# Strassen's seven block products in the second feed-forward layer

## The chip, the core and the metric

One core of a Trainium2 chip runs the program. Its engines work side by side, each from its own instruction stream, and meet through semaphores: TensorE (PE in the profile; PEld is its weight load) multiplies matrices into PSUM banks, VectorE (DVE) and ScalarE (ACT) do elementwise work, GpSimd (POOL) is nearly unused here, SyncE (SP) issues the weight loads. The metric is the device time of one execution in microseconds.

## The reference, cut to what matters

Two transformer stacks follow one another on 512 tokens of width 1024, all in fp32. The change is in the last feed-forward layer of the first stack:

```
h      = rms_norm(x) * gain              # [512, 1024]
gate   = h @ w_gate                      # [1024, 2816]
up     = h @ w_up                        # [1024, 2816]
hidden = silu(gate) * up                 # [512, 2816]
x      = x + hidden @ w_down             # [2816, 1024]
```

A final norm (`final_gain`) follows, and its output is the input of the second stack. Feed-forward layer 0 has the same shape and is not touched.

## The kernel before, in words

Activations are kept transposed: a tile is 128 features (the partitions) by 512 tokens. `x` and `h` have 8 tiles, `hidden` has 22 (FT). A weight block of 128 by 128 is the stationary operand, the tokens stream past it: one fp32 matmul of 512 columns (tokens), or of 256 for half of them. In the trace each fp32 matmul is two records, each with its weight load.

**Weights** come through a ring of 5 slots of 1 MB (`Ring`, L123, `Slot`, L108). SyncE issues the loads in order (L117), each as soon as the instruction that last read the slot has counted. A gate/up slot holds one tile: 8 blocks of the gate and 8 of the up projection. A down slot holds 16 blocks.

**Gate/up** is `GatedUnits` (L271). A unit is (tile, first token, last token): tiles 0 to 2 are done in two halves (6 units of 256 tokens), so that the low half can start before the high half of the norm is there, then tiles 3 to 21 with all 512 tokens. A unit is 16 matmuls (L295): 8 into a gate bank, 8 into an up bank, two such pairs of banks in turn. ScalarE takes Silu of the gate bank (L304) and VectorE multiplies by the up bank into `hidden` (L309). Unit u waits for the multiply of u - 2.

**Down** is `OutProjection` (L212): 10 units, 6 tiles of 512 tokens, then tiles 6 and 7 in their low and in their high half; 22 matmuls each (L254). VectorE adds each result to `x` (L268).

**Norms** (`Norm`, L140): for each unit of `x` ScalarE squares (L160), TensorE adds up over partitions with a matrix of ones (`sum`, L172), ScalarE takes the root (L182), VectorE a reciprocal and one refining step (`factor`, L188 to L196) and then 8 outputs (L202), low and high half of the tokens apart. The final norm's squares and sums run beside the down units; the factor of the low half starts after the ninth unit of ten (the sum of the eighth), the high half after the last.

The order of work is written out by hand, one stream for each engine. On TensorE the stretch ends

```
                    gate.unit(pe, 0)
                    norm.sum(pe, 11)
                    for n in range(1, len(gate.units)):
                        gate.unit(pe, n)
```

and `down_stage` then runs units 0 to 9 of the down projection, each followed by the norm sum of the unit before. VectorE runs the adds 0 to 8, `factor` and the outputs of the low half, add 9, and `factor` and outputs of the high half. When all is done, the second stack starts on every engine (at 1670.3 us of the profiled execution).

Of the kernel before, what the change touches and what calls it, by code (L numbers as in the profile page):

```python
# [13 lines left out]
P = 128  # L14
# [125 lines left out]
class Norm:  # L140
# [22 lines left out]
    def sum(self, pe, u):  # L163
        t, lo, hi = self.units[u]
        s = (self.number + u) % 4
        after(pe, self.squared, u)
        if t == 0 and self.chain.start:
            pe.wait_ge(self.chain.sem, self.chain.start)
        both = [(0, lo, hi)] if self.banks[0] == self.banks[1] else [(n, max(lo, i), min(hi, j)) for n, (i, j) in enumerate(SPANS)]
        for n, i, j in both:  # L170
            if i < j:
                m = pe.matmul(self.k.bank[:, self.banks[n], i:j], self.k.ones, self.squares[:, s, i:j],  # L172
                              start=(t == 0), stop=(t == self.tiles - 1))
        m.then_inc(self.summed.sem, 1)

# [95 lines left out]
class GatedUnits:  # L271


    def __init__(self, k, ring, norm, h, hidden, silu):
        self.k, self.norm, self.h, self.hidden, self.silu_ = k, norm, h, hidden, silu
        self.units = ([(t, 0, HALF) for t in range(3)] + [(t, HALF, SEQ) for t in range(3)]
                      + [(t, 0, SEQ) for t in range(3, FT)])
# [4 lines left out]
        self.slots = [ring.place((self.done, max(u for u in range(n) if self.units[u][0] == t))) for t in range(FT)]  # L282
# [23 lines left out]
    def multiply(self, v, u):  # L306
        t, lo, hi = self.units[u]
        after(v, self.silued, u)
        v.tensor_tensor(self.hidden[:, t, lo:hi], self.k.bank[:, 2 * (u % 2) + 1, lo:hi], self.silu_[:, u % 2, lo:hi],  # L309
                        ALU.mult).then_inc(self.product.sem, 1)  # L310

# [382 lines left out]
def first_block(k, x, h, a, constants, vectors, ctx_mod, sigmoid):  # L694

    vec = k.vec
    with ExitStack() as stack:
        ring = Ring(k, stack, 5, 100)
# [162 lines left out]
        norm3, gated1, down1 = ffn(out1, vec["norm_ffn1"], 38, {})  # L861
        norm4 = Norm(k, "final", x, KT, down1.units, [(down1.added, i) for i in range(10)], vec["final_gain"], x, (7, 6), temps, 50)
# [94 lines left out]
        with k.nc.Block(no_gpsimd_drain=True) as block:  # L957
            @block.sync
            def _(sp):
# [66 lines left out]
                for t in range(FT):  # L1026
                    gated1.slots[t].fetch(sp, a["gu1"][t])
                for i in range(11):
                    down1.slots[i].fetch(sp, a["down1"][i])
# [20 lines left out]
            def _(pe):  # L1050
                def mixer_end(out, norm, gate, group):
# [15 lines left out]
                    for i in range(8, 11):  # L1067
                        norm.sum(pe, i)
                    gate.unit(pe, 0)
# [51 lines left out]
                mixer_end(out0, norm1, gated0, ada_group)  # L1121
# [27 lines left out]
                mixer_end(out1, norm3, gated1, lambda n: None)  # L1149
                down_stage(down1, norm4, lambda: None)  # L1150
                norm4.sum(pe, 9)

            @block.scalar
            def _(e):
                def mixer_end(norm, gate):
# [6 lines left out]
                    norm.root(e, 1)  # L1162
                    for n in range(1, len(gate.units)):
                        gate.silu(e, n)

# [40 lines left out]
                mixer_end(norm1, gated0)  # L1206
                down_stage(norm2)
# [16 lines left out]
                down_stage(norm4)  # L1224
                norm4.root(e, 1)

            @block.vector
            def _(v):
                def mixer_end(out, norm, gate, group):
# [9 lines left out]
                    for t in range(KT):  # L1239
                        norm.out(v, 1, t)  # L1240
                    for n in range(1, len(gate.units)):
                        gate.multiply(v, n)
                        group(n)

# [75 lines left out]
                mixer_end(out0, norm1, gated0, ada_rows)  # L1320
# [43 lines left out]
                mixer_end(out1, norm3, gated1, lambda n: None)  # L1364
                down_stage(down1, norm4, lambda: None)
# [2185 lines left out]

def halves(w):
# [13 lines left out]
def layout(i):  # L3566
# [20 lines left out]
    for j in range(3):  # L3587
# [24 lines left out]
        "gu0": gu[0], "gu1": gu[1], "down0": stream(i["ffn_w_down"][0]), "down1": stream(i["ffn_w_down"][1]),  # L3612
# [21 lines left out]
```

## Time and profile before

| | |
|---|---|
| median of 3 runs | 3064.34 us (3064.19 to 3064.74) |
| profiled execution, span | 3059.0 us |
| instructions in it | 31313 |
| TensorE busy | 94% of the span |
| VectorE, ScalarE busy | 26%, 16% |

The profile is of one execution; its span runs from its first to its last instruction. The median of the runs stands 5.3 us above it. L is a line of the kernel. A group's row gives busy time, mean duration of one instruction in ns, and the engine's idle time before them with what ended it. Matmuls are pipelined, so their durations overlap.

### The profile page before, as it was taken

Reading aid. Unit: us, or ns where it says so; the run is one execution under the profiler, and the core shown is the slowest. Engines: PE = TensorE matmul, PEld = TensorE weight load, DVE = VectorE, ACT = ScalarE, POOL = GpSimd, SP = SyncE. Lnnn points to the kernel's source line nnn. Section 1 sums busy time; section 2 is a strip of 40 time slices with the busy share of each in tenths; the row PEclk is TensorE's granted clock in tenths of the full one; section 3 lists DMA queues with packets and bytes.
Section 4 is the critical chain, followed back from the end, with each engine's and each line's share of the span. In section 5 each row is a group of like instructions: output and inputs, shape, how many; then the busy total and the mean of one; then the engine's idle time right before and its main releaser. Section 6 shows DMA issues by size and latency. Waiting matters only on the chain. (4 is left out here: it accounts for less than half of the span.)

```text
span 3059.0 us, 31313 instructions
## 1 busy us (share of the span) xinstructions
PE 2888.6 (94%) x13580; PEld 1501.2 (49%) x13580; DVE 792.2 (26%) x1577; ACT 498.4 (16%) x1045; POOL 101.0 (3%) x90
## 2 busy tenths in 40 slices
PE   7998999999999999999998999789969989996998
PEld 4343475444455447544446745788623334432332
DVE  2325531010003233000002274555221231112113
ACT  2333310000001231000001231443110010001001
POOL 1000000000010010000000200010000000000000
PEclk9999999999999999999999999998989999997999
DMA  7211036545221111222111201100099953009994
GB/s 244 93 42 42 28 115 262 218 180 220 82 85 69 68 66 56 87 78 83 69 69 60 111 29 59 34 23 2 23 399 419 419 207 145 14 6 395 419 420 193
DMA packets 68577, 430.81 MB, mean 141 GB/s; under 512 B 8042, under 2 KB 8857, under 8 KB 21464
## 3 DMA queue, kind: packets, MB, share of 16 engines
q1 hardware_dynamic: 63640, 412.48, 34.5%
q0 software_dynamic: 4800, 16.33, 1.5%
q8 instruction: 107, 1.75, 0.2%
q14 instruction: 30, 0.25, 0.0%
HBM read 422.33 MB, written 13.79 MB: 143 GB/s over the span
## 5 line engine op out<-in xcount | busy, mean ns | idle before, releaser
L295 PE MATMUL bank<-h,weight_ring 128*128 128x512 f32 (+1 forms) x1600 | 608.3, 542 | 0.0
L295 PEld LDWEIGHTS bank<-h,weight_ring 128*128 128x128 f32 x1600 | 303.1, 190 | 300.3 <-issue 290.4
L254 PE MATMUL bank<-arena,weight_ring 128*128 128x512 f32 (+1 forms) x1264 | 422.9, 491 | 0.0
L254 PEld LDWEIGHTS bank<-arena,weight_ring 128*128 128x128 f32 x1264 | 238.1, 190 | 170.5 <-issue 154.5
L2151 PE MATMUL bank<-weight_ring,tokens_T 128*64 128x512 f32 x1024 | 231.8, 603 | 1.5 <-issue 1.5
L906 PE MATMUL bank<-h,weight_ring 128*128 128x512 f32 (+2 forms) x464 | 183.1, 547 | 5.2 <-DVE h L202 3.4
L2638 PE MATMUL bank<-h,weight_ring 128*128 128x256 f32 (+1 forms) x576 | 172.9, 457 | 8.5 <-ACT h L1933 8.5
L309 DVE TENSOR_TENSOR arena<-bank,arena 128x512 f32<-128x512 f32 (+1 forms) x50 | 31.4, 627 | 557.3 <-ACT arena L304 557.3
L3286 PE MATMUL bank<-h,weight_ring 128*128 128x512 f32 x384 | 166.6, 597 | 3.7 <-DMA weight_ring<-in_sc_in 3.7
L2151 PEld LDWEIGHTS bank<-weight_ring,tokens_T 128*64 128x64 f32 x1024 | 77.0, 139 | 153.0 <-issue 147.6
L2638 PEld LDWEIGHTS bank<-h,weight_ring 128*128 128x128 f32 x576 | 109.5, 192 | 70.6 <-issue 55.9
L906 PEld LDWEIGHTS bank<-h,weight_ring 128*128 128x128 f32 (+1 forms) x464 | 86.9, 193 | 96.2 <-issue 90.1
L304 ACT ACTIVATE arena<-bank 128x512 f32<-128x512 f32 (+1 forms) x50 | 27.3, 546 | 613.0 <-PE bank L295 613.0
L2190 PE MATMUL bank<-logits_or_select,h 128*128 128x512 f32 x256 | 118.7, 600 | 2.9 <-DVE logits_or_select L2311 2.9
L3286 PEld LDWEIGHTS bank<-h,weight_ring 128*128 128x128 f32 x384 | 73.5, 192 | 96.2 <-issue 91.2
L2174 PE MATMUL bank<-weight_ring,hidden_T 128*64 128x512 f32 x512 | 113.4, 595 | 3.4 <-DVE hidden_T L2299 3.1
L906 PE MATMUL bank<-weight_ring,h 128*128 128x512 f32 x256 | 113.5, 597 | 0.0
L268 DVE TENSOR_TENSOR x<-bank,x 128x256 f32<-128x256 f32 (+1 forms) x44 | 24.0, 545 | 338.0 <-PE bank L254 338.0
L160 ACT ACTIVATE arena<-x 128x512 f32<-128x512 f32 (+1 forms) x52 | 27.3, 530 | 387.4 <-DVE x L268 370.3
L400 DVE COPY arena<-bank 128x512 f32<-128x512 f32 x96 | 61.8, 685 | 93.5 <-PE bank L409 64.9
L906 PEld LDWEIGHTS bank<-weight_ring,h 128*128 128x128 f32 x256 | 47.6, 190 | 62.5 <-issue 58.7
L2318 DVE SCALAR_TENSOR_TENSOR x<-bank,vectors,x 128x512 f32<-128x512 f32 x80 | 60.1, 751 | 67.0 <-PE bank L2190 65.9
(387 smaller groups left out, 2633.0 us busy)
## 6 DMA issues: line engine op xcount, KB each, us to landing
weight_ring<-in_w_gate SPq DMA_DIRECT2D x64, 1024.0 KB, 25.0
weight_ring<-in_w_up SPq DMA_DIRECT2D x64, 1024.0 KB, 26.3
weight_ring<-in_w_down SPq DMA_DIRECT2D x64, 1024.0 KB, 26.1
arena<-in_ada_w SPq DMA_DIRECT2D x48, 1024.0 KB, 9.1
weight_ring<-in_gu SPq DMA_DIRECT2D x44, 1024.0 KB, 4.8
weight_ring<-in_down SPq DMA_DIRECT2D x22, 1024.0 KB, 4.8
weight_ring<-in_sc_in SPq DMA_DIRECT2D x12, 1024.0 KB, 12.2
weight_ring<-in_ev_in SPq DMA_DIRECT2D x8, 1024.0 KB, 6.9
```

The lines of the kernel that those rows point to most:

```text
L160: a.activation(self.squares[:, s, lo:hi], self.src[:, t, lo:hi] if src is None else src, ACT.Square, scale=(self.tiles * P) ** -0.5).then_ ...
L254: m = pe.matmul(bank, self.slots[i].buf[:, at * P:(at + 1) * P], self.src(c)[:, lo:hi], start=(c == 0), stop=(c == self.kt - 1))
L295: m = pe.matmul(self.k.bank[:, 2 * (u % 2) + p, lo:hi], self.slots[t].buf[:, at:at + P], self.h[:, c, lo:hi], start=(c == 0), stop=(c == K ...
L309: v.tensor_tensor(self.hidden[:, t, lo:hi], self.k.bank[:, 2 * (u % 2) + 1, lo:hi], self.silu_[:, u % 2, lo:hi], ALU.mult).then_inc(self.p ...
L400: v.tensor_copy(self.prob_T[:, c % 2, s, :], self.k.bank[:, 4 + s, :]).then_inc(self.copied.sem, 1)
L906: m = pe.matmul(out, lhs, rhs, start=(c == 0), stop=(c == last - 1))
L2151: m = pe.matmul(self.k.bank[e * CAP:(e + 1) * CAP, 3 + j, :], self.tok_T[:, r % 2, 4 * half + c, e * CAP:(e + 1) * CAP], slot.buf[:, c * D ...
L2174: m = pe.matmul(self.k.bank[e * CAP:(e + 1) * CAP, 6 + half, :], self.hid_T[:, 2 * fh + f, e * CAP:(e + 1) * CAP], slot.buf[:, at:at + 512 ...
L2190: m = pe.matmul(self.k.bank[:, 2 if n % 2 == 0 else 5, :], self.y[:, self.place(r), c * P:(c + 1) * P], self.sel[:, self.place(r), :], sta ...
L2318: v.scalar_tensor_tensor(self.x[:, c, :], self.k.bank[:, 2 if n % 2 == 0 else 5, :], self.gate[:, c:c + 1], self.x[:, c, :], ALU.mult, ALU ...
L2638: m = pe.matmul(self.bank(n)[:, 0:hi - lo], slot.buf[:, at:at + P], self.h[:, c, lo:hi], start=(c == 0), stop=(c == KT - 1))
L3286: last = pe.matmul(self.bank(m), self.slots[m // 2].buf[:, at:at + P], self.h[:, c, :], start=(c == 0), stop=(c == KT - 1))
```

## The change

Tiles 0 and 1 of gate/up stay as they are, in halves. For each of the other 20 tiles the two rows gate and up, the two halves of the inner dimension (4 blocks of 128 each) and the two halves of the tokens are a 2 by 2 block product, which is done in Strassen's form (Winograd's variant) with seven products instead of eight. Each product is 4 matmuls of 256 tokens. It needs sums of weight blocks (`sum_blocks`, VectorE, 4 operations of 128 x 512 a tile, one of them in place in the slot), sums of token blocks (`share`, once, 4 operations of 1024 elements on each partition) and sums of the products. "second" is accumulated onto "first" in its bank and "third" onto "fifth"; the other sums are VectorE's, with ScalarE's copies of "first" and "fifth" before. The tile's banks are 4 of the 8, the other 4 are the next tile's.

The down projection is done in the same form: 4 pairs of output tiles (p and p + 4), the inner dimension in 11 groups of two tiles, so each product is 11 matmuls of 256 tokens. Its token sums are made from `hidden` by `fold`, 4 operations of 256 elements for each pair of tiles. A pair's weights lie in three slots of 4, 4 and 3 groups (12 loads instead of 11, 11 MB as before); their block sums are VectorE's too. Most of the products' sums are added to `x` piece by piece (`take_sixth` and its like). In the last pair the order is another, and the last product is "third" alone. VectorE, ScalarE and TensorE get written orders of their own (`seven_stage`).

```diff
         self.k, self.norm, self.h, self.hidden, self.silu_ = k, norm, h, hidden, silu
-        self.units = ([(t, 0, HALF) for t in range(3)] + [(t, HALF, SEQ) for t in range(3)]
...
+                      + [(t, 0, SEQ) for t in range(halves, tiles_)])
         n = len(self.units)
...
+def sum_blocks(v, summed, i, slot, n, dst):
+    after(v, slot.turns, slot.i)
+    v.tensor_tensor(s1, a21, a22, ALU.add).then_inc(summed.sem, 1)
+    after(v, summed, 4 * i)
+    v.tensor_tensor(s2, s1, a11, ALU.subtract).then_inc(summed.sem, 1)
+    v.tensor_tensor(a21, a11, a21, ALU.subtract).then_inc(summed.sem, 1)
+    after(v, summed, 4 * i + 1)
+    v.tensor_tensor(s4, a12, s2, ALU.subtract).then_inc(summed.sem, 1)
...
+class SevenUp:
...
+    PAIRS = FT - 2
...
+        self.slots = [ring.place((self.done, m)) for m in range(n)]
...
+        return ("first", "sixth", "fifth", "seventh", "third", "second", "fourth")
...
+    def bank(self, m, name):
+        base = 4 if m % 2 == 0 else 0
+        place = {"first": 0, "second": 0, "fifth": 1, "third": 1, "sixth": 2, "seventh": 3, "fourth": 3}[name]
+        return self.k.bank[:, base + place, 0:HALF]
...
+    def room(self, pe, m, name):
+        if m == 1 and name == "first":
+            after(pe, self.halves.product, 3)
+        if m >= 2:
+            if name == "first":
+                after(pe, self.kept, 4 * (m - 2) + 3)
+            elif name == "sixth":
+                after(pe, self.combined, 7 * (m - 2))
+            elif name == "fifth":
+                after(pe, self.combined, 7 * (m - 2) + 3)
+            elif name == "seventh":
+                after(pe, self.combined, 7 * (m - 2) + 5)
+        if name == "second":
+            after(pe, self.kept, 4 * m)
+        elif name == "third":
+            after(pe, self.kept, 4 * m + 1)
+        elif name == "fourth":
+            after(pe, self.combined, 7 * m + 1)
...
+    def operands(self, pe, m, name):
...
+        if name == "sixth":
+            after(pe, self.summed, 4 * m + 1)
...
+            return sums[:, 512:1024], self.token_sums[1]
+        if name == "fifth":
+            return sums[:, 0:512], self.token_sums[0]
+        if name == "seventh":
+            after(pe, self.summed, 4 * m + 2)
...
+            return slot.buf[:, 1024:1536], self.token_sums[2]
+        if name == "third":
+            after(pe, self.summed, 4 * m + 3)
+            return sums[:, 1024:1536], self.h[:, 4:8, hi]
...
+    def product(self, pe, m, name):
+        self.room(pe, m, name)
+        left, right = self.operands(pe, m, name)
+        bank, onto = self.bank(m, name), name in ("second", "third")
+        for c in range(4):
+            last = pe.matmul(bank, left[:, c * P:(c + 1) * P], right[:, c, :], start=(c == 0 and not onto), stop=(c == 3), skip_group_check=onto)
...
+    def keep_fifth(self, a, m):
+        after(a, *self.made_at(m, "fifth"))
+        if m >= 2:
+            after(a, self.combined, 7 * (m - 2) + 4)
+        a.activation(self.temp(m, 2), self.bank(m, "fifth"), ACT.Copy).then_inc(self.kept.sem, 1)
...
+    def add_sixth(self, v, m):
+        after(v, *self.made_at(m, "sixth"))
+        after(v, self.kept, 4 * m)
+        v.tensor_tensor(self.temp(m, 0), self.bank(m, "sixth"), self.temp(m, 0), ALU.add).then_inc(self.combined.sem, 1)
...
+class SevenDown:
...
+        self.bank_free = (self.added, self.names.index((n - 2, "fourth")))
+        self.slots = []
+        for p in range(n):
+            last = self.order(p)[-1]
+            self.slots += [ring.place((self.slot_done, 2 * p)), ring.place((self.slot_done, 2 * p + 1)), ring.place(self.made_at(p, last))]
+
+    def order(self, p):
+        if p == self.PAIRS - 1:
+            return ("first", "sixth", "seventh", "second", "fourth", "fifth", "third")
+        return ("first", "sixth", "fifth", "seventh", "third", "second", "fourth")
...
+        elif name == "third":
+            if p == self.PAIRS - 1:
+                after(pe, *self.bank_free)
+            else:
+                after(pe, *self.added_at(p, "fifth"))
+        elif name == "fourth":
+            after(pe, self.combined, 2 * p + 1)
...
+        for j, (first, stop) in enumerate(DOWN_GROUPS):
+            q, n = 3 * p + j, (stop - first) * P
+            slot, sums = self.slots[q], self.sums[:, (self.up.PAIRS + q) % 3, :]
+            if name == "first":
+                slot.landed(pe)
...
+            if j < 2 and closing:
+                last.then_inc(self.slot_done.sem, 1)
+        last.then_inc(self.made.sem, 1)
...
+    def take_seventh(self, v, p):
+        after(v, *self.made_at(p, "seventh"))
+        after(v, self.combined, 2 * p)
+        v.tensor_tensor(self.temp(p, 1), self.bank(p, "seventh"), self.temp(p, 0), ALU.add).then_inc(self.combined.sem, 1)
...
+        gated1 = GatedUnits(k, ring, norm3, h, hidden, half_silu, 2, 2)
+        up1 = SevenUp(k, ring, h, hidden, token_sums, folded, block_sums, seven_temps, gated1)
+        down1 = SevenDown(k, ring, hidden, folded, block_sums, seven_temps, x, up1)
...
+                for m in range(up1.PAIRS):
+                    up1.slots[m].fetch(sp, a["gu1"][m + 2])
+                for i in range(12):
+                    down1.slots[i].fetch(sp, a["down1"][i, :, 0:down1.width(i)])
...
+                def seven_stage(gate, norm, up, down, following):
+                    gate.unit(pe, 0)
+                    norm.sum(pe, 11)
+                    up.product(pe, 0, "first")
+                    gate.unit(pe, 1)
+                    up.product(pe, 0, "second")
+                    gate.unit(pe, 2)
+                    gate.unit(pe, 3)
+                    for name in up.order(0)[2:]:
+                        up.product(pe, 0, name)
+                    for m in range(1, up.PAIRS):
+                        for name in up.order(m):
+                            up.product(pe, m, name)
+                    for p in range(down.PAIRS - 1):
+                        for name in down.order(p):
+                            down.product(pe, p, name)
+                    last = down.PAIRS - 1
+                    down.product(pe, last, "first")
+                    after(pe, *down.bank_free)
+                    for u in range(4):
+                        following.sum(pe, u)
+                    down.product(pe, last, "sixth")
+                    following.sum(pe, 4)
+                    following.sum(pe, 5)
+                    for name in ("seventh", "second", "fourth"):
+                        down.product(pe, last, name)
+                    following.sum(pe, 6)
+                    down.product(pe, last, "fifth")
+                    following.sum(pe, 7)
+                    down.product(pe, last, "third")
+                    following.sum(pe, 8)
+                    following.sum(pe, 9)
 
                 def ada_group(n):
                     if n >= 2 and n % 2 == 0:
...
+                def seven_stage(gate, up, down, following):
+                    up.keep_first(e, 0)
+                    for n in range(1, 4):
+                        gate.silu(e, n)
+                    for m in range(up.PAIRS):
+                        if m:
+                            up.keep_first(e, m)
+                        up.keep_fifth(e, m)
+                        up.silu_high(e, m)
+                        up.silu_low(e, m)
+                    down.keep_first(e, 0)
+                    down.keep_first(e, 1)
+                    following.square(e, 0)
+                    following.square(e, 1)
+                    down.keep_first(e, 2)
...
+                    for u in range(4, 8):
+                        following.square(e, u)
+                    following.root(e, 0)
+                    following.square(e, 8)
+                    following.square(e, 9)
+                    following.root(e, 1)
...
+                def seven_stage(gate, norm, up, down, following):
+                    up.share(v, norm)
+                    gate.multiply(v, 1)
+                    up.block_sums(v, 0)
+                    gate.multiply(v, 2)
+                    gate.multiply(v, 3)
+                    for m in range(up.PAIRS):
+                        up.add_sixth(v, m)
+                        if m + 1 < up.PAIRS:
+                            up.block_sums(v, m + 1)
+                        else:
+                            down.block_sums(v, 0)
+                        up.add_seventh(v, m)
+                        up.add_fifth(v, m)
+                        up.add_third(v, m)
+                        if m % 2 == 0:
+                            up.fold(v, m // 2)
+                        up.multiply_high(v, m)
+                        up.add_fourth(v, m)
+                        up.multiply_low(v, m)
+                    up.fold(v, FT // 2 - 1)
+                    down.block_sums(v, 1)
+                    down.block_sums(v, 2)
+                    for p in range(down.PAIRS - 1):
+                        down.take_sixth(v, p)
+                        down.take_fifth(v, p)
+                        down.take_seventh(v, p)
+                        down.take_third(v, p)
+                        for i in range(3):
+                            down.block_sums(v, 3 * (p + 1) + i)
+                        down.take_second(v, p)
+                        down.take_fourth(v, p)
+                    last = down.PAIRS - 1
+                    down.take_sixth(v, last)
+                    down.take_seventh(v, last)
+                    down.take_second(v, last)
+                    down.take_fourth(v, last)
+                    down.take_fifth(v, last)
+                    following.factor(v, 0)
+                    for t in range(KT):
+                        following.out(v, 0, t)
+                    down.take_third(v, last)
+                    following.factor(v, 1)
+                    for t in range(KT):
+                        following.out(v, 1, t)
 
```

## Rows read from the trace of the kernel before

**Rows 1.** The page: span, and busy us (share of the span) by engine.

```profile
span 3059.0 us, 31313 instructions
...
PE 2888.6 (94%) x13580; PEld 1501.2 (49%) x13580; DVE 792.2 (26%) x1577; ACT 498.4 (16%) x1045; POOL 101.0 (3%) x90
```

**Rows 2.** Busy time by stretch: gate/up from the last norm sum on; down projection.

```profile
core 0: us, PE busy (x) PEld busy (x) DVE busy (x) ACT busy (x) POOL busy (x), PEclk, DMA share, GB/s
1207.98:1503.44 295.46, 295.46 (x769) 145.92 (x768) 21.55 (x37) 15.85 (x27) 0.00 (x0) 1.00 0.21 75
1503.44:1660.77 157.33, 157.33 (x469) 88.93 (x468) 12.75 (x23) 7.27 (x12) 0.00 (x0) 1.00 0.13 47
```

**Rows 3.** Groups by form, 1207.5 to 1671: busy us, mean ns, idle before, releaser.

```profile
L295 PE MATMUL bank<-h,weight_ring 128*128 128x512 f32 x608 | 261.1, 592 | 0.0
L295 PEld LDWEIGHTS bank<-h,weight_ring 128*128 128x128 f32 x768 | 145.9, 190 | 149.1 <-issue 144.9
...
L254 PE MATMUL bank<-arena,weight_ring 128*128 128x256 f32 x176 | 38.6, 379 | 0.0
```

**Rows 4.** Timeline, VectorE: multiplies of wide units (start, us); 8 rows, first and last.

```profile
1257.07 0.69 DVE L309 TENSOR_TENSOR arena<-bank,arena 128x512 f32<-128x512 f32 x1 [13.52 <-ACT arena L304]
...
1353.20 0.69 DVE L309 TENSOR_TENSOR arena<-bank,arena 128x512 f32<-128x512 f32 x1 [13.04 <-ACT arena L304]
```

**Rows 5.** The same of half units; 4 rows, first and last.

```profile
1222.40 0.42 DVE L309 TENSOR_TENSOR arena<-bank,arena 128x256 f32<-128x256 f32 x1 [5.32 <-ACT arena L304]
...
1243.12 0.42 DVE L309 TENSOR_TENSOR arena<-bank,arena 128x256 f32<-128x256 f32 x1 [6.48 <-ACT arena L304]
```

**Rows 6.** Timeline at the first units, all engines.

```profile
1200.64 7.07 PE L295 MATMUL bank<-h,weight_ring 128*128 128x256 f32 x32
1207.54 0.59 PE L172 MATMUL bank<-arena,constants 128*128 128x256 f32 x2
...
1209.95 1.75 DVE L188 RECIPROCAL arena<-arena 128x256 f32<-128x256 f32 x1 [1.36 <-ACT arena L182]
...
1213.50 3.26 DVE L202 SCALAR_TENSOR_TENSOR h<-x,vectors,arena 128x256 f32<-128x256 f32 x8
```

**Rows 7.** Groups by form, 1207.5 to 1671, VectorE and ScalarE.

```profile
L309 DVE TENSOR_TENSOR arena<-bank,arena 128x512 f32<-128x512 f32 x19 | 13.1, 692 | 248.3 <-ACT arena L304 248.3
...
L304 ACT ACTIVATE arena<-bank 128x256 f32<-128x256 f32 x6 | 2.3, 383 | 36.0 <-PE bank L295 36.0
L268 DVE TENSOR_TENSOR x<-bank,x 128x256 f32<-128x256 f32 x4 | 1.7, 424 | 31.3 <-PE bank L254 31.3
...
L196 DVE TENSOR_TENSOR arena<-arena 128x256 f32<-128x256 f32 x3 | 1.3, 426 | 0.1
```

**Rows 8.** Groups on ScalarE, 1690 to 1750, in the second stack.

```profile
L2645 ACT ACTIVATE z_pool<-bank 128x256 f32<-128x256 f32 x16 | 6.1, 383 | 46.5 <-PE bank L2638 46.5
...
L2645 ACT ACT_TABLE_LOAD x1 | 1.3, 1283 | 0.0
```

**Rows 9.** DMA issues, 1445 to 1600: KB each, median us to landing.

```profile
weight_ring<-in_down SPq DMA_DIRECT2D x11, 1024.0 KB, 4.8
```

**Rows 10.** Timeline at the end of the stage, all engines.

```profile
1650.84 0.59 PE L172 MATMUL bank<-arena,constants 128*128 128x256 f32 x2
...
1651.98 1.75 DVE L188 RECIPROCAL arena<-arena 128x256 f32<-128x256 f32 x1 [0.51 <-ACT arena L182]
...
1655.54 3.26 DVE L202 SCALAR_TENSOR_TENSOR x<-x,vectors,arena 128x256 f32<-128x256 f32 x8
1660.77 0.59 PE L172 MATMUL bank<-arena,constants 128*128 128x256 f32 x2
1660.97 0.42 DVE L268 TENSOR_TENSOR x<-bank,x 128x256 f32<-128x256 f32 x1 [2.18 <-PE bank L254]
...
1670.32 2.19 ACT L1894 ACTIVATE delta_work<-x 128x512 f32<-128x512 f32 x4 [7.21 <-PEq L957]
```

More of the change, by code:

```diff
@@ L166, in sum @@
         after(pe, self.squared, u)
-        if t == 0 and self.chain.start:
+        if u == 0 and self.chain.start:
             pe.wait_ge(self.chain.sem, self.chain.start)
@@ L172, in sum, with final @@
                 m = pe.matmul(self.k.bank[:, self.banks[n], i:j], self.k.ones, self.squares[:, s, i:j],
-                              start=(t == 0), stop=(t == self.tiles - 1))
+                              start=(u == 0), stop=(u == self.final(n)))
         m.then_inc(self.summed.sem, 1)
+    def final(self, s):
+        lo, hi = SPANS[s] if self.banks[0] != self.banks[1] else (0, SEQ)
+        return max(u for u, (t, i, j) in enumerate(self.units) if i < hi and j > lo)
     def root(self, a, s):
@@ L281, in __init__ @@
         self.product = Turns(k.flag("gated_product"), n)
-        self.slots = [ring.place((self.done, max(u for u in range(n) if self.units[u][0] == t))) for t in range(FT)]
+        self.slots = [ring.place((self.done, max(u for u in range(n) if self.units[u][0] == t))) for t in range(tiles_)]
     def unit(self, pe, u):
@@ L1050, in _, with mixer_end @@
             def _(pe):
-                def mixer_end(out, norm, gate, group):
+                def mixer_end(out, norm):
                     for n in range(4):
@@ L1068, in mixer_end, with gated_stage @@
                         norm.sum(pe, i)
+                def gated_stage(gate, norm, group):
                     gate.unit(pe, 0)
@@ L1206, in _ @@
                 mixer_end(norm1, gated0)
+                gated_stage(gated0)
                 down_stage(norm2)
@@ L1240, in mixer_end, with gated_stage @@
                         norm.out(v, 1, t)
+                def gated_stage(gate, group):
                     for n in range(1, len(gate.units)):
@@ L3549, in stream, with quarters @@
     return tiles(w).transpose(1, 0, 2).reshape(P, -1, SLOT).transpose(1, 0, 2)
+def quarters(w):
+    t = tiles(w).reshape(2, KT // 2, P, FT // 2, 2, P)
+    out = np.zeros((KT // 2, 3, P, SLOT), np.float32)
+    for j, (first, stop) in enumerate(DOWN_GROUPS):
+        n = stop - first
+        blocks = t[:, :, :, first:stop].transpose(1, 2, 0, 4, 3, 5)
+        out[:, j, :, 0:4 * n * P] = blocks.reshape(KT // 2, P, 4 * n * P)
+    return out.reshape(-1, P, SLOT)
 def halves(w):
```

280 lines of the change are left out of this document (261 added, 19 removed).

## The prediction

> **What bounds the kernel now.** The page comes first: of a span of 3059.0 us TensorE is busy for 2888.6, VectorE for 792.2, ScalarE for 498.4 [rows 1]. TensorE sets the time wherever it is dense, so the next view is the table by stretch for the stage that the change rewrites: from the last norm sum before the second tile (1207.98) to the end of gate/up (1503.44), and from there to the last product of the down projection (1660.77) [rows 2]. TensorE is busy for all of 295.46 and all of 157.33 us, at a granted clock of 1.00 (the 2.4 GHz level); VectorE does 21.55 and 12.75 us, DMA is at 0.21 and 0.13. So the stage is matmul time and nothing else: a removed matmul is worth its full pitch, as long as the new work of VectorE and ScalarE keeps beside it.
>
> What is the pitch? An instruction's own duration (592 ns, or 379 at 256 columns) [rows 3] overlaps the next one's, so I take it from the evenly spaced multiplies of VectorE, one for each unit of 16 matmuls. Wide units of 512 columns: 96.13 us for 7 units, so 0.8583 us a matmul [rows 4]. Half units of 256 columns: 20.72 us for 3 units, so 0.4317 us a matmul [rows 5]. Each matmul is two records (608 for 19 tiles of 16) [rows 3], so a record takes 429 and 216 ns, with a weight load of 190 ns inside it. A half-width matmul costs 0.5030 of a wide one: the array's work counts, not the number of matmuls.
>
> **The change, part by part.** The window between the last norm sum (1207.98) and 1660.77 is 452.8 us. Before it holds 5 half units (80 matmuls at 256), 19 wide units (304), 6 wide down units (132) and 4 half down units (88 at 256).
> 1. *Removed:* 436 x 0.8583 + 168 x 0.4317 = 374.2 + 72.5 = 446.7 us. With 28 half-width records of norm sums (6.0 us) that is 452.7 of 452.8, so nothing else is in the window.
> 2. *Added:* 3 half units (48), 20 pairs of 7 products of 4 matmuls (560) and 4 pairs of 7 products of 11 (308), all at 256 columns: 916 x 0.4317 = 395.4 us. Sums 1 and 2: **-51.3 us**. Told otherwise: 1040 half-width matmuls become 916, which is 124 x 0.429 = 53.2 us; the half-width pitch is 2.5 ns above half of the wide one, and on the 748 that are new at this width it takes 1.9 back.
> 3. *Waits on TensorE.* Each of the 168 products begins with one to three waits, where before a unit had them every 16 or 22 matmuls. The trace of before has no group of 4 matmuls, so I bound this. Lower end: the first unit, whose first 8 matmuls each wait for one tile of the norm, runs 32 records in 7.07 us less one record's overhang of 0.16: 0.4317 us each, no loss [rows 6]. A met wait is free there. Upper end: if every product found its wait unmet, TensorE would drain (379 - 216 = 163 ns) and then load weights uncovered (190 ns), 0.353 us a product, 59.3 us in all. Which one holds is a question of lateness, taken next; I take 0, since the first unit is this very form (256 columns, waits before single matmuls).
> 4. *VectorE and ScalarE in a tile's 12.09 us (28 x 0.4317).* VectorE: four block sums at 512 elements (0.69 each, 0.72 with the dependent start), seven operations at 256 (0.42 to 0.43; 0.46 with the start), and on every second tile four folds: 2.9 + 3.2 + 0.9 = 7.0 us [rows 7]. It would have to be 1.7 times as slow to be the bound. ScalarE: four at 0.38. Copy, Silu and Square need no table load between them: 16 activations of the projection at line 2645, both Silu and Copy, ran with one load [rows 8]. Counted from a tile's start, product n ends at 1.73 n. The third product reuses the bank of the fifth: fifth ends at 5.18, ScalarE's copy is done at 5.18 + 0.2 + 0.4 = 5.8, the third product starts at 6.91, slack 1.1 us. The fourth product needs the bank of the seventh: VectorE finishes sixth and block sums at about 7.0, the seventh at 7.6, needed at 10.36, slack 2.8. The sums of the next tile are done 6 us ahead of need. So these cost 0 while covered by TensorE; the cover of the third product is the thin one.
> 5. *Start.* After the last norm sum TensorE has 4 + 16 + 4 matmuls (10.4 us) before it needs the high half of the norm instead of 32 (13.8). The first output of that half came 5.5 us after 1207.98 and the eighth at 1216.76 [rows 6], so cover remains. VectorE then does the four shared sums at 1024 elements, not in the trace: at least the 0.692 of 512, at most twice the rounded 1.39; the line through 256 and 512 gives 1.23, 4.9 us together. Multiply 1 ends near 1222.1, and the unit that waits for it starts at 1207.98 + 40 x 0.4317 = 1225.3: nothing lost even at 1.39 (1222.8). Cost 0.
> 6. *Up to down.* After tile 21's last product VectorE has add, multiply, four folds, then the block sums of the second slot: its second sum is there 4.1 us on; TensorE reaches it after 11 + 4 matmuls, 6.5 us. The third slot: 6.6 against 8.2. Cost 0.
> 7. *Slots of the down weights.* With 5 slots and 3 in a pair, the third slot of pair p + 1 is only freed when 7 matmuls of pair p remain (3.02 us). A load lands 4.8 us after issue [rows 9] (a 768 KB one somewhat less), so 1.4 to 2.1 us into the next pair; TensorE needs it at 3.45. But VectorE is in order: behind the block sums of that slot (2.4 us) stand the adds of "second" and "fourth". At pairs 1 and 2 nobody needs them soon. At the last pair TensorE stops after "first" (4.75 us) for exactly that add, done at 4.7 to 5.4. Range 0 to 0.7 here; I take **+0.4 us**.
> 8. *End.* Before, the sums of the low half end beside a unit of 22 matmuls, 9.5 us: norm sum at 1650.84, reciprocal from 1651.98, last low output ends 1658.80, which is 7.96 us after the sum; the last product ends at 1660.77 and its add starts 0.20 later [rows 10]. Now only "third" follows "fifth": 11 matmuls, 4.75 us. From the low sum S it ends at S + 5.18 and its add could start at S + 5.38, but VectorE, in order, is in the low outputs until S + 7.96. The add starts 2.6 us late, and the chain behind it (9.3 us to 1670.32) is the same: **+2.6 us**. Bounds: 0 if the outputs gave way, 2.6 by these rows.
>
> Sum: -51.3 + 0.4 + 2.6 = -48.3; span 3059.0 - 48.3 = 3010.7. The median of the runs, 3064.34, stands 5.3 us above the profiled span; 3010.7 + 5.3 = **3016.0 us**, 1.6% faster. A difference under 0.2% (6.1 us) could not be told from none.
>
> **The rivals.**
> *A, the forecast:* 3016.0, from 3014 to 3018 by the bounds of 7 and 8.
> *B, small lateness that repeats.* The slack of 1.1 us before "third" holds two semaphore hops and an activation. If each were late enough to miss by 0.4 us, 20 tiles lose 8 us; if pairs 1 to 3 also stall 1 us each on the third slot, 3 more: 3027. For it: all partial results pass through two in-order engines. Against: none of these engines is over 58% busy, and the rows show hops of 0.2 us.
> *C, less is lost:* neither the bank wait nor the end costs anything, 3013.0. Against it stands the order of VectorE's stream.
> *D, slower: the gaps between products.* Place: the first matmul of each of the 168 products. If a wait standing between two short groups keeps the next weights from being loaded ahead, each product pays up to 0.353 us, 3016.0 + 59.3 = 3075. It decides from 48.3 / 168 = 0.29 us a product. For it: weight loads fill 190 of the 216 ns of a record, so there is no room to catch up. Against: the first unit with its 8 waits shows none of it.
> *E, slower: loads that don't overlap.* After the change the window has 1832 records instead of 1208. If each load cost its 190 ns beside the product, the 624 more would add 118.6 us, and the time would be 3134. The rows speak against it: in the wide and in the half units the pitch (429, 216 ns) is the product's alone, though a 190 ns load lies in each.
> The Trainium skill, "TensorE: Matmul & The Clock Gate", Part 3 (The mechanism), states that a weight load overlaps a running matmul only where the row groups differ; all matmuls here use the whole array, so by that rule case E holds. By that rule, the trace does not agree.
>
> **How the numbers follow.** A 0.64, B 0.21, C 0.10, D 0.03, E 0.01, and 0.01 that losses of kind B grow until they eat the gain. Faster: 0.95; within 0.2%: 0.01; slower: 0.04. The range takes A, C and all of B: 3012.5 to 3027.
>
> **What would show it.** Right: in the new window TensorE busy throughout at clock 1.00, seven products a tile every 12.09 us (the multiplies of the low half equally spaced), weight loads busy for some 87% of it (1832 x 0.190 / 401), no idle time of TensorE behind VectorE or ScalarE but a few tenths once before the final norm sums, and VectorE's add of "third" starting 2.8 us after the product's end. Window 401.8 instead of 452.8. B: idle time on the first matmul of "third" or "fourth", 20 times. D: an idle gap of 0.2 to 0.35 us at every product's start. E: a pitch above 0.216 us a record. The forecast is wrong if the tile's period is over 12.3 us or the end costs more than 3 us.

## The result and the profile after

The changed kernel takes **3015.51 us** (median of 4 runs, 3014.30 to 3016.81), the kernel before 3064.27 us beside it: a ratio of 0.9839, 95% interval 0.9825 to 0.9853. The forecast was 3016.0. That the two agree within 0.5 us is partly luck, as shown below; the rewritten stretch itself is the better test, since its length can be read from the trace to a tenth.

The page of the changed kernel, the rows that answer to [rows 1], then the busy time by stretch, to be held against [rows 2]:

```profile
span 3015.0 us, 33212 instructions
...
PE 2842.3 (94%) x14204; PEld 1624.8 (54%) x14204; DVE 944.2 (31%) x1899; ACT 518.6 (17%) x1108; POOL 101.0 (3%) x90
```

```profile
core 0: us, PE busy (x) PEld busy (x) DVE busy (x) ACT busy (x) POOL busy (x), PEclk, DMA share, GB/s
1206.79:1473.20 266.41, 266.41 (x1236) 234.53 (x1235) 140.83 (x291) 35.53 (x87) 0.00 (x0) 1.00 0.25 86
1473.20:1608.24 135.04, 135.04 (x627) 118.87 (x626) 42.59 (x86) 7.76 (x15) 0.00 (x0) 1.00 0.14 50
1206.79:1608.24 401.45, 401.45 (x1861) 353.40 (x1860) 183.41 (x376) 43.29 (x102) 0.00 (x0) 1.00 0.21 74
```

TensorE is again busy in every microsecond, at the same granted clock, and the window has shrunk from 452.8 to 401.45 us. VectorE's work went from 34 to 183 us and weight loads now fill 353.40 of 401.45 us (88%); neither shows in the time. What TensorE still waits for between the window's start and the second stack is one row, the norm sum at the very end:

```profile
engine line waited for: us in total, times, longest us
PE bank L172 <- ACT arena L160: 3.0, 1, 3.0
```

Here is one tile in the timeline. Line 419 holds the matmuls of the products (x8 is one product of 4 matmuls, x16 is two), 437 is ScalarE's copy of "fifth" and 476 VectorE's add of "seventh". The tile begins with "first" at 1239.60; the third row of TensorE is "third", the fourth "fourth", and the last is "first" of the next tile:

```profile
1239.60 1.89 PE L419 MATMUL bank<-h,weight_ring 128*128 128x256 f32 x8
...
1241.33 3.62 PE L419 MATMUL bank<-h,arena 128*128 128x256 f32 x16
...
1244.98 0.38 ACT L437 ACTIVATE arena<-bank 128x256 f32<-128x256 f32 x1 [3.07 <-PE bank L419]
...
1246.51 1.89 PE L419 MATMUL bank<-h,arena 128*128 128x256 f32 x8
1246.71 0.42 DVE L476 TENSOR_TENSOR arena<-bank,arena 128x256 f32<-128x256 f32 x1 [0.50 <-PE bank L419]
...
1249.96 1.89 PE L419 MATMUL bank<-arena,weight_ring 128*128 128x256 f32 x8
...
1251.69 1.89 PE L419 MATMUL bank<-h,weight_ring 128*128 128x256 f32 x8
```

A product starts every 1.73 us and the tile takes 1251.69 - 1239.60 = 12.09 us. The copy of "fifth" ends at 1245.36, 1.15 us before "third" begins (1246.51); the add of "seventh" ends at 1247.13, 2.83 us before "fourth" (1249.96).

The end of the stage, to be held against [rows 10]:

```profile
1603.06 0.59 PE L172 MATMUL bank<-arena,constants 128*128 128x256 f32 x2
...
1604.20 1.75 DVE L192 RECIPROCAL arena<-arena 128x256 f32<-128x256 f32 x1 [0.18 <-ACT arena L186]
...
1607.76 3.26 DVE L206 SCALAR_TENSOR_TENSOR x<-x,vectors,arena 128x256 f32<-128x256 f32 x8
1608.24 0.59 PE L172 MATMUL bank<-arena,constants 128*128 128x256 f32 x2
1610.93 0.42 DVE L664 TENSOR_TENSOR x<-bank,x 128x256 f32<-128x256 f32 x1
...
1611.85 1.22 PE L172 MATMUL bank<-arena,constants 128*128 128x256 f32 x2 [3.01 <-ACT arena L160]
...
1620.79 0.63 POOL L3263 MEMSET state<- 128x640 f32 x1 [521.92 <-POOLq L1359]
```

The last product ends at 1608.24, but VectorE is in the low half's outputs (L206) until 1610.9 and only then does the last add (L664), 2.69 us behind the product. The norm sum behind it takes 1.22 us. In the kernel before it took 0.70, after 0.53 us of idling:

```profile
1661.90 0.70 PE L172 MATMUL bank<-arena,constants 128*128 128x256 f32 x2 [0.53 <-ACT arena L160]
```

### The profile page after: what moved, and what is told of

It reads as the page before. It is cut to its first block and busy times, and to the rows that moved or that the text cites. A ratio compares the mean times of both kernels' runs of the same rounds, so it can differ in the third digit from the quotient of the medians.

```text
span 3015.0 us, 33212 instructions
## 1 busy us (share of the span) xinstructions
PE 2842.3 (94%) x14204; PEld 1624.8 (54%) x14204; DVE 944.2 (31%) x1899; ACT 518.6 (17%) x1108; POOL 101.0 (3%) x90
## 5 line engine op out<-in xcount | busy, mean ns | idle before, releaser
L299 PE MATMUL bank<-h,weight_ring 128*128 128x512 f32 (+1 forms) x928 | 333.8, 520 | 0.0
L258 PE MATMUL bank<-arena,weight_ring 128*128 128x256 f32 (+1 forms) x824 | 270.1, 483 | 0.0
L299 PEld LDWEIGHTS bank<-h,weight_ring 128*128 128x128 f32 x928 | 175.4, 190 | 153.6 <-issue 145.4
L258 PEld LDWEIGHTS bank<-arena,weight_ring 128*128 128x128 f32 x824 | 154.5, 190 | 104.6 <-issue 93.3
L3153 PEld LDWEIGHTS bank<-h,weight_ring 128*128 128x128 f32 x576 | 109.9, 193 | 71.6 <-issue 57.0
L3801 PEld LDWEIGHTS bank<-h,weight_ring 128*128 128x128 f32 x384 | 73.6, 192 | 96.4 <-issue 91.4
L419 PE MATMUL bank<-h,arena 128*128 128x256 f32 x480 | 110.1, 379 | 0.0
L313 DVE TENSOR_TENSOR arena<-bank,arena 128x512 f32<-128x512 f32 (+1 forms) x29 | 17.4, 599 | 292.3 <-ACT arena L308 292.3
L419 PEld LDWEIGHTS bank<-h,arena 128*128 128x128 f32 x480 | 91.2, 190 | 12.4
```

Source lines behind the costliest of these rows:

```text
L258: m = pe.matmul(bank, self.slots[i].buf[:, at * P:(at + 1) * P], self.src(c)[:, lo:hi], start=(c == 0), stop=(c == self.kt - 1))
L299: m = pe.matmul(self.k.bank[:, 2 * (u % 2) + p, lo:hi], self.slots[t].buf[:, at:at + P], self.h[:, c, lo:hi], start=(c == 0), stop=(c == K ...
L419: last = pe.matmul(bank, left[:, c * P:(c + 1) * P], right[:, c, :], start=(c == 0 and not onto), stop=(c == 3), skip_group_check=onto)
L3153: m = pe.matmul(self.bank(n)[:, 0:hi - lo], slot.buf[:, at:at + P], self.h[:, c, lo:hi], start=(c == 0), stop=(c == KT - 1))
L3801: last = pe.matmul(self.bank(m), self.slots[m // 2].buf[:, at:at + P], self.h[:, c, :], start=(c == 0), stop=(c == KT - 1))
```

## The experiments

For each run the table gives the length of the **stage** (from the start of the norm sum ahead of the second unit to the start of the second stack), the part of it after the last product, and the **rest** of the profiled execution (span less stage). Stage, end and rest are of that one execution; the median is of all.

| kernel | median, us | stage | its end | rest |
|---|---|---|---|---|
| before | 3064.27 | 462.77 | 9.54 | 2596.2 |
| before_again (one run) | 3064.60 | 462.77 | 9.55 | 2600.0 |
| changed | 3015.51 | 414.43 | 12.55 | 2600.6 |
| after_again | 3016.43 | 414.30 | 12.42 | 2600.5 |
| up_only | 3032.31 | 429.76 | 9.54 | 2601.0 |
| before_halves | 3062.27 | 464.29 | 9.54 | 2596.0 |
| vector_3_more | 3017.20 | 414.94 | 12.54 | 2600.2 |
| vector_6_more | 3040.34 | 435.58 | 12.54 | 2601.8 |
| scalar_5_more | 3038.56 | 436.16 | 12.02 | 2602.4 |
| tail_add_early | 3011.70 | 412.06 | 10.18 | 2595.9 |
| tail_sum_early | 3012.85 | 411.42 | 9.54 | 2595.2 |
| tail_both | 3010.76 | 411.42 | 9.54 | 2597.8 |
| tail_both_again | 3010.74 | 411.42 | 9.54 | 2597.4 |

The stage repeats to 0.13 us, while the rest varies over 7 us. So small effects are read from the stage.

The rest is not wholly free of the kernel, though. Every execution has its span on record; less the stage of the table, which is taken as fixed, the median rest is 2599.0, 2599.5 and 2600.8 us for the kernel before in three groups of 9 to 13 executions, and 2599.2 and 2600.4 for the changed kernel. But it is 2596.2 for before_halves (10 executions, 2595.1 to 2598.2) with 2599.5 for the kernel before in the same rounds, and 2597.5 and 2597.4 for tail_both in its two sets. Neither edit touches code outside the stage, so why these rests are shorter is not known, and a difference of medians of 2 or 3 us says nothing of the stage.

**One part of the change alone: up_only.** The down projection goes back to `OutProjection` and its old orders:

```diff
-        down1 = SevenDown(k, ring, hidden, folded, block_sums, seven_temps, x, up1)
+        down1 = OutProjection(k, ring, FT, lambda c: hidden[:, c, :], once(lambda pe, c: after(pe, gated1.product, 3) if c < 2 else after(pe, up1.combined, 7 * (c - 2) + 6)),
+                              x, 6, down_banks, {0: [(up1.combined, 7 * 18 + 6)], 1: [(up1.combined, 7 * 18 + 6)]})
...
-                        if m % 2 == 0:
-                            up.fold(v, m // 2)
```

> The down projection is put back as it was (10 units of 22 matmuls, 6 of them 512 tokens wide); gate/up keeps the seven products. Count theory: the window from the last norm sum before the second unit to the last product holds 48 + 560 half-width matmuls and 132 wide and 88 half-width ones of the old down projection: 262.5 + 113.3 + 38.0 + 6.0 (sums) = 419.8 us, against 401.4 measured with both parts. The wait at the end is gone (VectorE's last add starts 0.2 us after the last product, not 2.7). Together about +15.5 us over the changed kernel, 3031. Rival (most of the gain sits in one part, or the short products of the up part pay hidden gaps that the long ones of the down part don't): the window is off 419.8 by several us.

Measured 3032.31 us (ratio to before 0.9896, 0.9881 to 0.9911). The stretch that was forecast at 419.8 us, in the columns of the table by stretch above:

```profile
1208.68:1628.47 419.79, 419.79 (x1686) 319.96 (x1685) 134.40 (x263) 42.32 (x98) 0.00 (x0) 1.00 0.20 71
```

The count of matmuls gives each part's share: gate/up 452.8 - 419.8 = 33.0 us, down 419.8 - 401.45 = 18.3 us, of which the longer end takes 3.0 back. Both shares are what the matmuls alone make, so neither the short products (4 matmuls) nor the long ones (11) pay anything beyond them; the rival falls.

**Width alone: before_halves.** All gate/up tiles of the kernel before in halves, no Strassen (the waits of the down projection are renumbered to match):

```diff
-                      + [(t, 0, SEQ) for t in range(3, FT)])
+                      + ([(t, i, j) for t in range(3, FT) for i, j in SPANS] if split else [(t, 0, SEQ) for t in range(3, FT)]))
```

> The kernel before, with all tiles of gate/up in two halves of 256 tokens: 608 half-width matmuls in place of 304 wide ones, same arithmetic, twice the weight loads, no Strassen. Pitch theory: 608 x 0.4317 - 304 x 0.8583 = +1.6 us over the kernel before. Rival E (weight loads don't overlap in full): 608 more records at up to 0.19 us, up to +115 us. Rival D (a wait before a short group costs a gap): 19 more unit starts at up to 0.35 us, +7 us.

The stage grew by 1.52 us (464.29 - 462.77). The medians can't tell it (ratio 0.9994, 0.9984 to 1.0003); they even stand 1.8 us the other way, which is the shorter rest told above. There are twice the weight loads and 304 matmuls more, and the cost is 2.5 ns for each of the 608 half-width matmuls. That puts rival E out, and rival D as far as waits ahead of 16 matmuls go; for groups of 4 the changed kernel itself shows no gap. The records and loads of this kernel:

```profile
L295 PE MATMUL bank<-h,weight_ring 128*128 128x256 f32 x1387 | 299.7, 379 | 0.0
L295 PEld LDWEIGHTS bank<-h,weight_ring 128*128 128x128 f32 x1385 | 263.3, 190 | 35.7
```

1387 matmul records in 299.7 us, 216 ns each, with 190 ns of load inside every one.

**How much VectorE can take: vector_3_more and vector_6_more.** `n` is 3 or 6:

```diff
+                        for i in range(n):
+                            if m or i:
+                                after(v, extra, n * m + i - 1)
+                            v.tensor_tensor(scratch, h[:, 0, 0:512], h[:, 1, 0:512], ALU.add).then_inc(extra.sem, 1)
                         up.add_seventh(v, m)
```

> Three more VectorE operations of 512 elements in each of the 20 tiles, ahead of the add of seventh (they write a scratch tile nobody reads), each behind the one before: 3 x 0.72 = 2.16 us a tile. Slack theory (TensorE needs the bank of seventh only 2.8 us after VectorE has freed it): no change in the tile's 12.09 us, whole stage as before, 3015.5. Rival (VectorE's work is already felt, by order or by memory ports): each tile grows by part of 2.16, up to +43 us in all.

The stage is 0.51 us longer where the forecast was 0, with 43 us of work added. Beside the one at the end, TensorE's waits name one place:

```profile
PE bank L419 <- DVE arena L476: 0.3, 1, 0.3
PEld bank L419 <- DVE arena L476: 0.7, 1, 0.7
```

It is the first tile, whose order is another: "second" was done early there, "fourth" follows "third" at once and the slack before it is 1.7 us less. The forecast had overlooked that tile. The other 19 hide it all, so for them the rival (VectorE's work is felt already) falls.

> Six more such operations, 4.32 us a tile: the add of seventh then ends 11.35 us after the tile's start, fourth can start at about 11.45 instead of 10.36. Slack theory: a tile takes 13.2 us instead of 12.09, +22 us over 20 tiles, 3037, with the idle time of TensorE all before fourth. Rival (VectorE is loaded to 58% and its total counts, not the order): 7.0 + 4.3 = 11.3 us still fits into 12.09 and nothing changes.

The stage is 21.2 us longer (forecast 22), the time 3040.34 us. The order decides, not the load, since the 11.3 us of work that the forecast counts would have fitted into a tile. TensorE's waits, and the place in one tile:

```profile
PE bank L419 <- DVE arena L476: 15.8, 20, 2.4
```

```profile
1307.13 0.42 DVE L476 TENSOR_TENSOR arena<-bank,arena 128x256 f32<-128x256 f32 x1
1307.60 1.99 PE L419 MATMUL bank<-arena,weight_ring 128*128 128x256 f32 x8 [0.70 <-DVE arena L476]
1307.60 1.59 PEld L419 LDWEIGHTS bank<-arena,weight_ring 128*128 128x128 f32 x8 [1.11 <-DVE arena L476]
...
1309.43 1.89 PE L419 MATMUL bank<-h,weight_ring 128*128 128x256 f32 x8
```

This also prices rival D. When the wait is unmet, that is, when TensorE arrives before the add is done, "fourth" starts 0.05 us after the add's end. Its weight load starts with it and not ahead of it, and the next product follows after 1.83 us instead of 1.73. So beside the lateness itself an unmet wait costs 0.05 + 0.10 = 0.15 us. That is well below the upper bound of 0.353 and the 0.29 at which the sign would have turned, and it is paid only on products that are late.

**How much ScalarE can take: scalar_5_more.**

```diff
+                        after(e, *up.made_at(m, "fifth"))
+                        for i in range(5):
+                            if m or i:
+                                after(e, extra, 5 * m + i - 1)
+                            e.activation(scratch[:, 0:HALF], h[:, 0, 0:HALF], ACT.Copy).then_inc(extra.sem, 1)
                         up.keep_fifth(e, m)
```

> Five more ScalarE copies of 256 elements in each tile between the end of fifth and the copy of its bank, each behind the one before: 5 x 0.44 = 2.2 us. The slack before third is 1.15 us in the trace of the changed kernel. Slack theory: third starts 1.1 us late in each tile, 13.2 us a tile, +22 us in all, 3037. Rival (the thin slack is not what TensorE waits on): less than +5 us.

The stage is 21.7 us longer (forecast 22), the time 3038.56 us. Two copies of "first" one tile apart, and the wait of TensorE:

```profile
1311.39 0.38 ACT L431 ACTIVATE arena<-bank 128x256 f32<-128x256 f32 x1 [3.07 <-PE bank L419]
...
1324.59 0.38 ACT L431 ACTIVATE arena<-bank 128x256 f32<-128x256 f32 x1 [3.07 <-PE bank L419]
```

```profile
PE bank L419 <- ACT arena L437: 16.9, 20, 0.8
```

13.20 us a tile, as forecast; every one of the 20 tiles waits before "third". The slack of 1.1 us is real. It is the thinnest in the 19 regular tiles; in the first tile that before "fourth" is as thin.

**The end: tail_add_early, tail_sum_early, tail_both.** The first changes only VectorE's order:

```diff
                     following.factor(v, 0)
-                    for t in range(KT):
+                    for t in range(2):
                         following.out(v, 0, t)
                     down.take_third(v, last)
+                    for t in range(2, KT):
+                        following.out(v, 0, t)
```

> Only the order of VectorE at the end changes: the last add (of the product third) comes after two of the eight low outputs instead of after all eight; the other six run while ScalarE and TensorE make the root of the high half. Theory (the end is set by VectorE's order): the add starts 0.3 us after the last product instead of 2.7, the reciprocal of the high half 8.4 us after the start of the low half's last norm sum instead of 10.6: about 2.1 us less, 3013.4. Rival (the end is set by the chain root, reciprocal, outputs anyway): no change, 3015.5.

The stage is 2.37 us shorter (median 3011.70).

```profile
1607.20 0.59 PE L172 MATMUL bank<-arena,constants 128*128 128x256 f32 x2
1607.51 0.42 DVE L664 TENSOR_TENSOR x<-bank,x 128x256 f32<-128x256 f32 x1
1607.85 2.45 DVE L206 SCALAR_TENSOR_TENSOR x<-x,vectors,arena 128x256 f32<-128x256 f32 x6
...
1608.43 0.70 PE L172 MATMUL bank<-arena,constants 128*128 128x256 f32 x2 [0.63 <-ACT arena L160]
1609.17 0.47 ACT L186 ACTIVATE arena<-bank,constants 128x256 f32<-128x256 f32 x1 [0.79 <-PE bank L172]
1610.22 1.74 DVE L192 RECIPROCAL arena<-arena 128x256 f32<-128x256 f32 x1
```

The add starts 0.31 us after the product. The root is there at 1609.64, and VectorE, with its six outputs, comes to the reciprocal 0.6 us later: the rest of the loss.

The second moves the low half's last norm sum into "fifth" (the new argument is called after the first 4 of its 11 matmuls) and the factor ahead of the take of "fifth":

```diff
-                    down.product(pe, last, "fifth")
-                    following.sum(pe, 7)
+                    down.product(pe, last, "fifth", lambda: following.sum(pe, 7))
...
-                    down.take_fifth(v, last)
                     following.factor(v, 0)
+                    down.take_fifth(v, last)
```

> In the last pair the last norm sum of the low half is put inside the product fifth, after 4 of its 11 matmuls, and VectorE makes the factor of the low half before it takes fifth. Theory: the low half's sum starts 3.0 us earlier against the last product, VectorE is busy until about 11.0 us after the end of fourth, the last add starts 0.65 us after the last product instead of 2.7: 2.0 us less, 3013.5. Rival: ScalarE or the add of fifth holds it up as long as before: 3015.5.

```profile
1606.90 0.59 PE L172 MATMUL bank<-arena,constants 128*128 128x256 f32 x2
1607.11 0.42 DVE L666 TENSOR_TENSOR x<-bank,x 128x256 f32<-128x256 f32 x1
```

The stage is 3.01 us shorter, 1.0 more than forecast. The add starts 0.21 us after the product and not 0.65, since the two adds of "fifth" and the eight outputs took 3.9 us, where I had 4.2. The other half of the surplus is the last norm sum, 0.70 us again instead of the changed kernel's 1.22. The end is back at 9.54 us, that of the kernel before.

> Both changes of the end together (the last add after six of the eight low outputs). Theory: the last add 0.2 to 0.3 us after the last product, and the reciprocal of the high half 2.2 us behind it with VectorE free by then: 2.5 us from the order and up to 0.5 from TensorE's clock, which in the changed kernel was low for the last norm sum after 3.0 us of idling; 3.0 us less, 3012.5. Rival: the two gains are the same one and tail_both is no better than the better of the two.

411.42 us, the same as tail_sum_early: the rival holds, the two gains are one. Its ratio to before is 0.9825 (0.9812 to 0.9838).

**The same kernels again: after_again, before_again, tail_both_again.**

> The changed kernel once more, unaltered. Theory (what lies outside the stage differs from one execution to the next, whatever the kernel): the stage, from the last norm sum before the second unit to the start of the second stack, takes 414.4 us again within 0.5, while the rest of the program, 2600.6 us in the first profile of this kernel and 2596.2 in that of the kernel before, comes out elsewhere between the two. Rival (the change itself slows the second stack by 5.5 us): 1394.2 us after the stage again, as in the first profile, within 0.5.

> The kernel before, unaltered. Same theories: the stage 462.8 us again; the second stack 1388.7 us by the rival, and anything from 1388 to 1395 by the theory.

> The version with both changes at the end, on the same chip and in the same rounds as the changed kernel: stage 411.4 us against 414.4, median 3.0 us under that of the changed kernel, as far as the scatter of 2 to 3 us of single runs lets it be seen.

The stages came again within 0.13 us (414.30, 462.77, 411.42). The forecast for the rest was met in part: the changed kernel's came again almost to the tenth (2600.5 after 2600.6), and it was the kernel before that moved, from 2596.2 to 2600.0. From the stage's end to the end of the span the kernel before took 1388.7 us in its first profile and 1392.3 in the second, the changed one 1394.2 and 1392.6; the rival had both repeat within 0.5. So most of the second stack's extra 5.5 us in the first pair of profiles was the executions, and the median rests of the two kernels (2599.0 to 2600.8, 2599.2 and 2600.4) show nothing left for the change. In the same rounds the version with both changes ran at 3010.74 us and the changed kernel at 3016.43. Of these 5.7 us the stage explains 2.9; the rest of it lies outside the stage and is not explained.

## Why the prediction was right

By its own steps:

1. and 2. *The count.* Forecast 452.8 to 401.4 us, -51.3; measured 401.45, -51.3. Pitch times count was the whole of it, and up_only and before_halves confirm the two halves and the 2.5 ns of width apart.
3. *Waits.* Taken at 0, found at 0: no wait of TensorE inside the window. The bound of 0.353 us for an unmet one was far too high, 0.15 is shown.
4. *VectorE and ScalarE.* The slacks of 1.1 and 2.8 us are 1.15 and 2.83 in the trace, and the two loads that exceed them cost 21.7 and 21.2 us of the 22 forecast. The step's gap was the first tile, with its own order; in the changed kernel it costs nothing.
5. *Start.* The four shared sums took 1.22 us each (1.23 from the line through the two known lengths). Nothing was lost.
6. *Up to down.* No wait, as forecast.
7. *Slots.* Forecast +0.4, measured 0:

```profile
1570.66 0.56 DVE L324 TENSOR_TENSOR arena<-weight_ring 128x384 f32<-128x384 f32 x1 [5.51 <-DMA weight_ring<-in_down]
...
1572.67 0.75 DVE L664 TENSOR_TENSOR x<-bank,x 128x256 f32<-128x256 f32 x2
...
1573.71 3.62 PE L172 MATMUL bank<-arena,constants 128*128 128x256 f32 x16
```

VectorE did wait 5.5 us for the slot and the two adds stood behind it, but they ended at 1573.42, 0.3 us before TensorE was through with "first". The mechanism was there, on the good side of its range.

8. *End.* Forecast +2.6, measured +3.0 (9.54 to 12.55; 12.42 in after_again). That is at the prediction's own mark for being wrong, an end that costs more than 3 us: 3.01 here, 2.88 there. The add was 2.69 us behind the product against 0.20 before, 2.5 us; the other 0.5 is TensorE's clock. Its granted clock while it idled and in the norm sum that followed:

```profile
1608.80:1611.80 3.00, 0.04 (x1) 0.00 (x0) 2.55 (x7) 0.42 (x1) 0.00 (x0) 0.98 0.00 0
1611.80:1613.20 1.40, 1.22 (x2) 0.50 (x2) 0.00 (x0) 0.09 (x1) 0.00 (x0) 0.50 0.00 0
```

After 3.0 us without a matmul the two matmul records ran at the 1.2 GHz level, 0.5 us slower. The same idling in scalar_5_more left the clock at 1.00:

```profile
1636.80:1637.70 0.90, 0.70 (x2) 0.30 (x2) 0.00 (x0) 0.11 (x2) 0.00 (x0) 1.00 0.00 0
```

There the sum took 0.70 us (its end is 12.02), so the drop does not come every time: of the five profiles with this gap three have 0.50 and 1.22 us (changed, vector_3_more, vector_6_more), after_again has 0.61 and 1.09, and one has none. The prediction had named the late add but not this price.

*The sum.* -51.3 + 0 + 3.0 = -48.3, as forecast, from two terms that were each off by 0.4 in opposite directions. That the total hits to the tenth is luck; the -51.3 is not. One figure beside the sum was not derived as said: rival A was given as 3014 to 3018 us "by the bounds of 7 and 8", but those bounds (0 to 0.7 and 0 to 2.6) give 3013.0 to 3016.3.

*From span to median.* This step was weak. I added 5.3 us for what lies around the span. In the profiled run of the changed kernel the span is 3015.0 and the time 3016.81, and in the repeat of the kernel before 3062.8 and 3064.60: 1.8 us. The other 3.5 of the 5.3 were a fast second stack in the one profile I had (1388.7 us against 1392.3 in the repeat). It did no harm, because a difference from the median of before was what was wanted, and that carries over whatever the 5.3 consists of.

Of the rivals, B (repeated lateness) did not occur; its mechanism exists and begins 1.1 us further on. C came half true: the bank wait cost nothing, the end did. D and E are refuted: here 190 ns loads lie inside 216 ns records with all rows in use. The Trainium skill, "TensorE: Matmul & The Clock Gate", Part 3 (The mechanism), has a rule that loads overlap only where row groups differ, and by that rule the trace does not agree. The same section also lets a load into the background weight buffer run ahead of running matmuls; with that the trace agrees, though no run here shows which buffer a load went to.

What stays open: why the second stack takes 1389 to 1394 us from one execution to the next, and why the rest is some 3 us shorter in before_halves and tail_both. No run was aimed at either.

## What to carry to other kernels

Where TensorE is dense, take the pitch of each width from evenly spaced consumers and count matmuls; an algorithm that saves products is then worth its count, as long as each bank's release has slack in the order of the engine that releases it, which decides long before that engine's load does. Look at the last step separately: a shorter last product uncovers work of an in-order engine that the longer one hid, and a reduction placed inside the product before it brings that back (here 3.0 us beside a gain of 51, half a microsecond of it by the clock). And compare stages rather than spans when an effect is smaller than the scatter of the rest.

## What the runs showed that was not expected

An unmet wait ahead of a group of 256-column matmuls costs, beside the lateness itself, only 0.05 us from the end of the awaited instruction and 0.10 us of uncovered weight load. After 3.0 us of idling TensorE's clock fell to half for the next two matmul records in three profiles of five (0.50, 1.22 us instead of 0.70), in part in one, and stayed up in one. And doubling the number of weight loads in a dense stage, to 190 of every 216 ns, cost 1.5 us in 262.
